# A gated state-space mixer: four gate units and part of two normalisations move into the last scan steps, and each scan step is written unit, broadcasts, outputs

## What is computed

```python
y_f, st_f = ssd_chunked(xh, dt[:, :, 0], A[0], bm, cm, h0_f)      # scan, 4 chunks x 4 groups, forward
y_b, st_b = ssd_chunked(rev(xh), rev(dt[:, :, 1]), ...)           # and backward
y = y_f + rev(y_b) + d_skip * xh
z, uv, gate_a, gate_b = split_cols(xm_l @ w_in, ...)              # 1024 + 2048 + 1024 + 1024 columns
g = y * silu(z)                                                   # the gate
ssd = rmsnorm(g in 4 groups of 256 columns, norm_w)
u, v = split(gelu(uv))
v = layernorm(v, ln_w, ln_b)
sgu = u * (w_s @ v per chunk and group + b_s)                     # 8 groups of 128 columns
merged = sigmoid(gate_a) * (ssd @ w_pa) + sigmoid(gate_b) * (sgu @ w_pb)
h = h + g1 * (merged @ w_o)
```

## Time and profile before

| what | value |
|---|---|
| median of three runs | 3422.75 us (3421.1 to 3422.89) |
| profiled execution: its time, its span | 3426.89 us, 3425.2 us |
| PE matmul busy | 3266.0 us (95%) |
| DVE busy | 1559.3 us (46%) |
| ACT busy | 668.6 us (20%) |
| POOL busy | 154.9 us (5%) |
| mean granted TensorE clock | 0.985 of 2.4 GHz |

### The profile page before, as it was taken

How to read it: one execution, slowest core, us unless ns; L and a number is a source line. 1 busy time by engine, 2 the same in 40 slices (tenths; PEclk the granted TensorE clock), 3 DMA queues, 4 the chain that set the end, 5 groups by cost and what they waited for, 6 DMA issues and landing times. The chain is left out here.

```text
span 3425.2 us, 37926 instructions
## 1 busy us (share of the span) xinstructions
PE 3266.0 (95%) x14833; PEld 2317.0 (68%) x14833; DVE 1559.3 (46%) x2453; ACT 668.6 (20%) x1108; POOL 154.9 (5%) x159
## 2 busy tenths in 40 slices
PE   8999999999999999999999999899989999999897
PEld 7888844588887888854488887555754887433332
DVE  4554356455436554348355534424336655322122
ACT  2111015111102111014221101531553100200001
POOL 1000001000000000001000000100330000000000
PEclk9999999999999999999999999999999999999999
DMA  6333321333243332422223231322113235799998
GB/s 156 86 98 106 118 62 43 89 88 87 80 136 92 86 86 86 142 57 56 80 74 88 84 126 47 95 79 80 44 31 89 78 111 198 294 421 421 421 421 334
DMA packets 421963, 460.00 MB, mean 134 GB/s; under 512 B 33722, under 2 KB 393645, under 8 KB 397004
## 3 DMA queue, kind: packets, MB, share of 16 engines
q1 hardware_dynamic: 418592, 452.23, 39.4%
q10 hardware_dynamic: 1452, 1.67, 0.4%
q0 software_dynamic: 1792, 4.35, 0.3%
HBM read 450.12 MB, written 7.86 MB: 134 GB/s over the span
## 5 line engine op out<-in xcount | busy, mean ns | idle before, releaser
L497 PE MATMUL psum<-arena 128*128 128x256 f32 x7392 | 1610.8, 380 | 6.5 <-DVE arena L898 6.5
L497 PEld LDWEIGHTS psum<-arena 128*128 128x128 f32 x7392 | 1399.6, 190 | 219.7 <-issue 14.4
L971 DVE TENSOR_TENSOR arena<-arena 128x512 f32<-128x512 f32 (+2 forms) x152 | 94.6, 623 | 750.0 <-PE psum L497 730.2
L2505 PE MATMUL psum<-arena 128*64 128x512 f32 x1536 | 345.7, 596 | 27.9 <-DMA arena<-in_w_gate_dram 12.8
L2505 PEld LDWEIGHTS psum<-arena 128*64 128x64 f32 x1536 | 112.9, 136 | 250.2 <-issue 247.7
L1764 PE MATMUL psum<-arena 128*128 128x256 f32 x1120 | 243.0, 379 | 1.4 <-DVE arena L2169 1.4
L1764 PEld LDWEIGHTS psum<-arena 128*128 128x128 f32 x1120 | 211.7, 189 | 32.7 <-DVE arena L2169 1.8
L769 ACT COPY arena<-psum 128x256 f32<-128x256 f32 x104 | 38.8, 373 | 824.5 <-PE psum L497 824.5
L624 PE MATMUL psum<-arena 128*128 128x512 f32 x416 | 185.6, 599 | 9.1 <-DVE arena L1106 6.3
L624 PEld LDWEIGHTS psum<-arena 128*128 128x128 f32 x416 | 77.9, 192 | 108.9 <-issue 100.9
L1584 PE MATMUL psum<-arena 128*128 128x512 f32 x320 | 141.3, 594 | 2.5 <-ACT arena L1790 1.7
(11 more groups left out here) (427 smaller groups left out, 2758.4 us busy)
## 6 DMA issues: line engine op xcount, KB each, us to landing
arena<-in_w_gate_dram SPq DMA_DIRECT2D x64, 1024.0 KB, 26.7
arena<-in_w_up_dram SPq DMA_DIRECT2D x64, 1024.0 KB, 26.6
...
arena<-in_ffn_w_gate_dram SPq DMA_DIRECT2D x88, 512.0 KB, 5.0
arena<-in_ffn_w_up_dram SPq DMA_DIRECT2D x88, 512.0 KB, 5.1
...
```

The costliest lines, as they stand in the source:

```text
L497: mm = pe.matmul(psum[:, b0 + b, c:c + HT], w, right(x), start=(first and c == 0), stop=last, skip_group_check=True)
L971: dve.tensor_tensor(sv[:, 0, :, :], a21, a22, ALU.add)
L2505: mm = pe.matmul(psum[64 * e:64 * e + 64, bank0 + half, :], x[:, k, 64 * e:64 * e + 64], ring[(n + e) % SLOTS][:, r, half * 512:(half + 1) ...
```

## The change

Three things. (1) In each scan step PE runs the unit first, then `bcasts(n+1)`, then `outputs(n)`; DVE runs `combine(n)` before `masked(n+1)`; ACT runs the gelu or silu before `decay_matrices(n+1)`. (2) z units 0 to 3 become the units of steps 12 to 15; their silu (`silu_z`) goes to ACT in the same steps, into a new tile `z_early` that lies in the third joint weight slot; `gate_y(0)` and `gate_y(1)` go into steps 14 and 15. SP therefore loads three pairs of z weights ahead of the layer norm's weights instead of one, and joint unit 0's weights wait for `gate_y(3)` (`z_ok` 4). (3) The sums, the centring and the squares of v go into steps 10 to 15, two token tiles at a time, and the tail is put in a new order.

```diff
@@ -1298,6 +1298,11 @@
         sq_v = x_flat[:, 1024:2048]
         mixed = x_flat[:, 2048:3072].rearrange("p (s t) -> p s t", s=2)
         z_s = df.rearrange("p s h i -> p s (h i)")
+        z_early = arena[:, wsum_at + 3072:wsum_at + 5120].rearrange("p (s t) -> p s t", t=T)
+
+        def z_at(n):
+            return z_early[:, n, :] if n < 4 else z_s[:, n % 2, :]
+
 
...
@@ -1415,7 +1420,7 @@
                 slot_free(VP + n // 2, n % 2)
                 load(n % 2, 256, [of("w_in_2", VC + 256 * n, 0, 0, 256)])
             single(UB, 2, UC + 512)
-            single(ZP, 1, ZC)
+            single(ZP, 3, ZC)
 
             sp.wait_ge(s["y_used"], 16)
...
@@ -1427,13 +1432,14 @@
                     sp.wait_ge(unit_done, JOINT + u)
                 else:
                     sp.wait_ge(s["xbc_ready"], 12 + 16)
+                    sp.wait_ge(s["z_ok"], 4)
...
             joint_load(0, "w_in_2", GA)
-            single(ZP + 1, 3, ZC + 256)
+            single(ZP + 3, 1, ZC + 768)
             for u in range(1, 16):
...
@@ -1697,8 +1703,6 @@
 
             bcasts(0)
             for n in range(NT * G):
-                if n + 1 < NT * G:
-                    bcasts(n + 1)
                 if n < 8:
                     v_half(n)
                 elif n < 12:
@@ -1706,6 +1710,10 @@
                         pe.wait_ge(s["vh_free"], 4)
                         pe.wait_ge(bank_free[1], UB + 1)
                     unit(UB * 2 + n - 8, xm)
+                else:
+                    unit(ZP * 2 + n - 12, xm)
+                if n + 1 < NT * G:
+                    bcasts(n + 1)
                 outputs(n)
...
@@ -1733,13 +1741,19 @@
                     mm = pe.matmul(bank(6 + q % 2), ones256, sq_y[:, 2 * q + t, :], start=(t == 0), stop=(t == 1))
                 mm.then_inc(s["gvar_done"], 1)
 
-            for n in range(8):
-                unit(ZP * 2 + n, xm)
-                if n >= 5:
-                    group_var(n - 5)
-                if n >= 4:
-                    mix(2 * (n - 4))
-                    mix(2 * (n - 4) + 1)
+            unit(ZP * 2 + 4, xm)
+            unit(ZP * 2 + 5, xm)
+            group_var(0)
+            group_var(1)
+            mix(0)
+            mix(1)
+            unit(ZP * 2 + 6, xm)
+            mix(2)
+            mix(3)
+            unit(ZP * 2 + 7, xm)
+            group_var(2)
+            for g in range(4, 8):
+                mix(g)
             pe.wait_ge(bank_free[0], MERGE + 1)
             pe.wait_ge(bank_free[1], MERGE + 1)
 
@@ -1875,10 +1889,18 @@
                                               bias=nacum[:, c, at:at + 1])
                     last.then_inc(s[ready], 1)
 
+            def silu_z(n):
+                act.wait_ge(unit_done, ZP * 2 + n + 3)
+                if n >= 6:
+                    act.wait_ge(s["z_ok"], n - 1)
+                act.activation(z_at(n), bank(n % 2), ACT.Silu).then_inc(bank_free[n % 2], 1)
+
+            def square_y(n):
+                act.wait_ge(s["z_ok"], n + 1)
+                act.activation(sq_y[:, n, :], y[:, n, :], ACT.Square).then_inc(s["y_sq"], 1)
+
             decay_matrices(0)
             for n in range(NT * G):
-                if n + 1 < NT * G:
-                    decay_matrices(n + 1)
                 if n < 8:
                     at, half = n // 2, n % 2
                     if half:
@@ -1890,34 +1912,41 @@
                        .then_inc(bank_free[at % 2] if half else s["vh_free"], 1)
                 elif n < 12:
                     u_out(UB * 2 + n - 8, n - 4)
+                else:
+                    silu_z(n - 12)
+                if n >= 14:
+                    act.wait_ge(s["v_mean"], 1)
+                    for t in (2 * n - 28, 2 * n - 27):
+                        act.activation(sq_v, v_tok[:, t, :], ACT.Square, accum_out=v_var[:, t:t + 1])
+                        act.drain()
                 if n == 8:
                     act.drain()
                     act.sem_inc(s["v_gelu"], 1)
+                if n + 1 < NT * G:
+                    decay_matrices(n + 1)
             act.wait_ge(s["ws_tr"], 1)
             for r in range(2):
                 last = act.copy(ws_T[:, 4 * r:4 * r + 4, :].rearrange("p a b -> p (a b)"), bank(2 + r))
             last.then_inc(s["ws_ok"], 1)
-            act.wait_ge(s["v_mean"], 1)
-            for t in range(NT):
-                if t:
-                    act.drain()
-                last = act.activation(sq_v, v_tok[:, t, :], ACT.Square, accum_out=v_var[:, t:t + 1])
-            act.drain()
             act.activation(v_var, v_var, ACT.Sqrt, scale=1.0 / 1024, bias=eps6).then_inc(s["v_std"], 1)
             def group_std(q):
                 act.wait_ge(s["gvar_done"], q + 1)
                 act.activation((rs_y if q < 2 else rs_y2)[:, q % 2, :], bank(6 + q % 2), ACT.Sqrt, bias=eps6)\
                    .then_inc(s["gstd"], 1)
 
-            for n in range(8):
-                act.wait_ge(unit_done, ZP * 2 + n + 3)
-                if n >= 2:
-                    act.wait_ge(s["z_ok"], n - 1)
-                act.activation(z_s[:, n % 2, :], bank(n % 2), ACT.Silu).then_inc(bank_free[n % 2], 1)
-                act.wait_ge(s["z_ok"], n + 1)
-                act.activation(sq_y[:, n, :], y[:, n, :], ACT.Square).then_inc(s["y_sq"], 1)
-                if n >= 5:
-                    group_std(n - 5)
+            for n in range(4):
+                square_y(n)
+            silu_z(4)
+            silu_z(5)
+            group_std(0)
+            group_std(1)
+            square_y(4)
+            square_y(5)
+            silu_z(6)
+            silu_z(7)
+            group_std(2)
+            square_y(6)
+            square_y(7)
             group_std(3)
             for u in range(20):
                 act.wait_ge(unit_done, JOINT + u + 3)
@@ -2119,27 +2148,31 @@
                                                     op0=ALU.mult, op1=ALU.add)
                 last.then_inc(s["y_used"], 1)
 
+            def gate_y(n):
+                dve.wait_ge(bank_free[n % 2], ZP + n // 2 + 2)
+                dve.tensor_tensor(y[:, n, :], y[:, n, :], z_at(n), ALU.mult).then_inc(s["z_ok"], 1)
+
             masked(0)
             for n in range(NT * G):
                 if n:
                     skip(n - 1)
+                combine(n)
                 if n + 1 < NT * G:
                     masked(n + 1)
-                combine(n)
+                if n in (10, 11):
+                    t = 2 * n - 20
+                    dve.wait_ge(s["v_gelu"], 1)
+                    dve.tensor_reduce(v_sum[:, t:t + 2], v_tok[:, t:t + 2, :], AX.X, ALU.add)
+                    dve.drain()
+                    dve.tensor_scalar(v_sum[:, t:t + 2], v_sum[:, t:t + 2], 1.0 / 1024, None, ALU.mult)
+                if n in (12, 13):
+                    for t in (2 * n - 24, 2 * n - 23):
+                        last = dve.tensor_scalar(v_tok[:, t, :], v_tok[:, t, :], v_sum[:, t:t + 1], None, ALU.subtract)
+                    if n == 13:
+                        last.then_inc(s["v_mean"], 1)
+                if n >= 14:
+                    gate_y(n - 14)
             skip(NT * G - 1)
-
-            dve.wait_ge(s["v_gelu"], 1)
-            dve.tensor_reduce(v_sum, v_tok, AX.X, ALU.add)
-            dve.drain()
-            dve.tensor_scalar(v_sum, v_sum, 1.0 / 1024, None, ALU.mult)
-            dve.drain()
-            for t in range(NT):
-                last = dve.tensor_scalar(v_tok[:, t, :], v_tok[:, t, :], v_sum[:, t:t + 1], None, ALU.subtract)
-            last.then_inc(s["v_mean"], 1)
-
-            def gate_y(n):
-                dve.wait_ge(bank_free[n % 2], ZP + n // 2 + 2)
-                dve.tensor_tensor(y[:, n, :], y[:, n, :], z_s[:, n % 2, :], ALU.mult).then_inc(s["z_ok"], 1)
 
             def gate_u(g):
                 dve.wait_ge(s["mix_done"], g + 1)
@@ -2199,10 +2232,8 @@
                 dve.tensor_tensor(out[:, 2:4, :], out[:, 3:4, :].to_broadcast([128, 2, HT]), ps[:, 3:5, :],
                                   ALU.add).then_inc(s["collected0" if m == 0 else "collected1"], 1)
 
-            gate_y(0)
-            for k in range(4):
-                right_sums(xm, xm_sum, k, "xm_sums")
-            gate_y(1)
+            gate_y(2)
+            gate_y(3)
             dve.wait_ge(s["v_std"], 1)
             dve.reciprocal(v_var, v_var)
             dve.wait_ge(s["ln_in"], 48)
@@ -2210,18 +2241,29 @@
             for t in range(NT):
                 dve.scalar_tensor_tensor(out=v_tok[:, t, :], in0=v_tok[:, t, :], scalar=v_var[:, t:t + 1],
                                          in1=ln_w, op0=ALU.mult, op1=ALU.mult)
-            gate_y(2)
-            weight_sums(0)
-            gate_y(3)
             dve.drain()
             dve.tensor_tensor(v_tok, v_tok, ln_b.unsqueeze(1).to_broadcast([128, NT, 1024]), ALU.add)\
                .then_inc(s["v_ok"], 1)
-            for n in range(4, 8):
-                gate_y(n)
-                gate_u(2 * (n - 4))
```

(23 more changed lines are left out.)

## The result

The changed kernel takes 3398.3 us (median of 6 runs, 3395.53 to 3401.78) against 3422.44 (6 runs): the ratio is 0.9931, interval 0.992 to 0.9941. The profiled execution took 3395.53 us with a span of 3393.8; that is 31 us under the profiled one of before, while the medians differ by 24. The runs of the changed kernel lie 6 us apart, and the part ahead of the scan alone was 3.7 us shorter in this execution (2401.54 against 2405.23), so I compare traces from the start of the scan.

The account below looks back on a forecast made before the run. PE was busy for 95% of the span, the last chain shared by transfers (7%) and PE (7%). Savings of 27.9 - 0.4 - 1.2 = 26.3 us from 3422.75 gave 3396.5 us, range 3390.5 to 3405.

Parts of the forecast that it names:

- Savings reach the end: Experts behind the mixer: their stream starts earlier with the joint units, so savings ahead of joint unit 0 count in full.
- Term 1, the scan: Scan: no stalls, steps of 10.86 us, all sixteen with a unit, 174.3 us in all, ending 4.0 us earlier.
- The tight step: Step 14 of the scan, where ACT also squares two tiles of v; `outputs(15)` still hidden, by 0.4 us.
- Term 2, the tail: Tail: DVE's serial queue, not PE, starts joint unit 0 at 46.9 us into it, 27.9 us earlier than before.
- A late load: Scan or tail: DVE or chain longer, or late `ln` load; 8 us lost, 3404.5, with both 3410; chance 0.14.
- Term 3, the debt: Joint units 0 to 2: DVE's remaining work holds back joint unit 3, losing 0.4 us once.
- Term 4, the clock: Near the tail's end: three PE waits bring one spell of lower clock, costing 1.2 us.
- Work costed at nothing: Scan and tail: sums and centring of v on DVE, and SP's three weight loads ahead of z units, cost nothing.

Follow-up runs that it names:

- e6: The changed kernel with three extra DVE operations of 128x512 inside `combine(n)`, the chain about 2.3 us longer in every step: 3400.7 us, ratio 0.9932.
- e7: The changed kernel with eight extra DVE operations inside `combine(n)`, the chain about 6.1 us longer in every step: 3453.5 us, ratio 1.0087.
- e4: The changed kernel with the sums, centring and squares of v put back into the tail: 3403.4 us, ratio 0.9943.
- e3: The changed kernel with DVE's tail reordered: four `right_sums` of xm before the wait for the layer norm's weights, `weight_sums(0)` ahead of `gate_u(4)`: 3391.5 us, ratio 0.9911.
- e8: The changed kernel with the layer norm waiting only for its own two loads, the third on a semaphore of its own: 3397.3 us, ratio 0.9921.
- e11: The changed kernel with four idle matmuls on PE between `mix(5)` and `mix(6)` in the tail: 3395.0 us, ratio 0.9922.
- e2: The changed kernel with the old order inside each scan step on PE, DVE and ACT, the moved work kept: 3407.2 us, ratio 0.9953.
- e5: The changed kernel with the old order inside each scan step on DVE and ACT, PE alone keeping the new one: 3484.3 us, ratio 1.0173.
- e10: The kernel of e3 with `norm_y(1)` moved from behind `gate_u(3)` to behind `gate_u(5)`: 3393.7 us, ratio 0.9919.
- e1: The kernel before with only the new order inside each scan step, no work moved out of the tail: 3409.3 us, ratio 0.996.
- e12: The kernel of e3 with `weight_sums(0)` moved ahead of `gate_u(2)`: 3390.4 us, ratio 0.9911.

## Why the prediction was right

Predicted 3396.5, measured 3398.3, inside the range. The two terms that make the gain, the scan and DVE's queue in the tail, came as described; the term of the clock did not, and the closeness of the sum is in part luck. By its steps:

- **Savings reach the end.** Right: 26.5 us less up to joint unit 19, 1.1 us less behind it.
- **Term 1, the scan.** Right: 173.9 us for 174.3, steps of 10.82 for 10.86. e6 and e7 place the slack: 2.3 us more hide in all steps but the first and the last, 6.1 us more cost 3.1 a step. The tight step was the one named (e4), but 0.3 us of wait came where I had 0.4 of slack. The `ScalarE` timeline of step 14 (silu, table load, first exp) has the pieces:

```profile
2562.66 0.60 ACT L1896 ACTIVATE arena<-psum 128x512 f32<-128x512 f32 x1 [2.78 <-PE psum L1590]
...
2565.63 1.28 ACT L1882 ACT_TABLE_LOAD   x1
...
2566.93 0.60 ACT L1882 ACTIVATE arena<-psum 128x512 f32<-128x512 f32 x1
```

From the end of the silu's wait to the exps it is 4.27 us, with 1.30 for the switch, not 2.66. The Trainium skill, "ScalarE: Activation LUTs", section What ACT_TABLE_LOAD costs, gives about 2.66 us for every switch; by it, as an estimate, this step would hold 1.4 us more. The trace does not show it.

- **Term 2, the tail.** The mechanism was right, DVE's queue and the third load: e3, e4 and e8 each move the tail by moving the start of the layer norm or what stands behind it, and in e11 the tail followed the landing of the load. In size, the queue behind the layer norm is 38.9 us where I had 39.2. The load was mis-sized for the profiled execution: 9.45 us into the tail instead of 7.7. In e2, e5, e6, e7 and e11 it was 7.7 to 7.8, so both occur; how often, and how much of the spread of the runs it makes, is not shown. A late load stands among the prediction's rivals, at 8 us; it came at 1.7. PE's waits were 4.07 and 0.70 where I had 2.1, 0.5 and 1.9.
- **Term 3, the debt.** Right in kind, e10 shows it; in the changed kernel itself it is near nothing (J0-2 are 38.35 us against 38.28), where I had 0.4.
- **Term 4, the clock.** Wrong. The window shows the spell that I foresaw:

```profile
2618.00:2622.00 4.00, 2.50 (x11) 2.50 (x12) 3.85 (x7) 0.63 (x1) 0.00 (x0) 0.68 0.00 0
```

but its price of 1.2 us is not there, since PE waits for DVE in that stretch whether its mixes are fast or slow. I priced a slow spell by PE's work in it, without asking whether PE bounded the stretch. Where the spell reaches into joint unit 0 (e4, e5, e7) it costs 1.6 to 2.1 us, so the price was one of two outcomes and not impossible. The size was also read wrongly: the spell near 2556 of the kernel before runs from 2554.8 to 2561.7, which would be 3.4 us; 1.7 fits the shorter ones near 2566 and 2576. And 1.7 less 0.4 is 1.3, not 1.2. It nearly made up for the late load, which I had not counted: the sum of 26.3 us met the trace's 26.5 by two errors of 1.2 and 1.7 us with opposite effect. (A slip that changes nothing here: two losses of 8 us each make 3412.5, where the rival has 3410.)
- **Work costed at nothing.** Right for SP's order (no unit waits for weights). Putting the norm's work into the scan is worth 5 us by the medians and 7 by the traces (e4), 2 of the latter through the clock in joint unit 0.
- **Left open**: what sets the spread of the runs, 3395.5 to 3401.8 us for the changed kernel, 3420.3 to 3422.9 for the first six of before and 3418.7 to 3431.3 for the 42 measured beside e1 to e12. The stretch ahead of the scan, whose code is the same, differs by up to 6.7 us between profiled executions (scan start 2401.3 in e1 to 2408.05 in e8).
